# A Conformer convolution taken in two halves of 256 tokens, with the first half's layer norm and projection placed inside the second half's blocks

## The reference, cut to what matters

```python
hn = rms_norm(h, norm1_g[1])
u = hn @ w_pw1 + b_pw1                              # 1024 -> 2048
u = u[..., :1024] * jax.nn.sigmoid(u[..., 1024:])   # the gate
u = depthwise_conv(u, w_dw, width 31, causal) + b_dw
m, var = mean and variance of u over the 1024 channels of a token
u = (u - m) * lax.rsqrt(var + 1e-5) * ln_g + ln_b   # layer norm
u = silu(u)
h = h + u @ w_pw2 + b_pw2                           # the projection
```

## Time and profile before

| | |
|---|---|
| median of 3 runs | 1392.17 us |
| the profiled execution's own time | 1388.63 us |
| its span in the trace | 1386.9 us |
| granted TensorE clock, mean over the span | 0.931 of full |
| TensorE matmuls busy | 1145.5 us, 83% of the span |
| VectorE busy | 538.4 us, 39% |
| ScalarE busy | 382.7 us, 28% |
| GpSimd busy | 248.7 us, 18% |
| bytes moved by DMA | 271.85 MB |

### The profile page before, as it was taken

How to read it: one execution, slowest core, us unless ns; L and a number is a source line. 1 busy time by engine, 2 the same in 40 slices (tenths; PEclk the granted TensorE clock), 3 DMA queues, 4 the chain that set the end, 5 groups by cost and what they waited for, 6 DMA issues and landing times.

```text
span 1386.9 us, 27835 instructions
## 1 busy us (share of the span) xinstructions
PE 1145.5 (83%) x11810; PEld 624.7 (45%) x11810; DVE 538.4 (39%) x951; ACT 382.7 (28%) x727; POOL 248.7 (18%) x250
## 2 busy tenths in 40 slices
PE   5978889999999889869987882999449869988781
PEld 2345556555555464535544441444114535544440
DVE  6833545544545432331111114489971231111114
ACT  3223243334333312211111112355551211111112
POOL 2000000000000000412221110388820412221210
PEclk9999999999999999969999996999769979999996
DMA  6042110110101333489999996326200489999985
GB/s 157 3 49 4 52 51 7 47 29 26 51 6 48 148 131 111 168 331 421 420 421 422 422 385 251 109 61 218 101 0 20 153 345 421 421 421 422 422 358 206
DMA packets 149115, 271.85 MB, mean 196 GB/s; under 512 B 62178, under 2 KB 106210, under 8 KB 131584
## 3 DMA queue, kind: packets, MB, share of 16 engines
q1 hardware_dynamic: 136960, 240.68, 46.1%
q0 software_dynamic: 10880, 21.00, 4.0%
q10 hardware_dynamic: 1152, 8.39, 1.5%
HBM read 263.73 MB, written 23.07 MB: 207 GB/s over the span
## 4 chain that ended last, share of the span: by engine, by line
PE 61%; DMA 15%; DVE 9%; POOL 4%; issue 4%; SPq 4%; ACT 2%; POOLq 0%; DVEq 0%; ACTq 0%
PE psum L1212 13%; DMA big<-in_moe_w_up_dram 11%; PE psum L807 11%; PE psum L1685 8%; PE psum L1398 5%; POOL big L1888 4%; PE psum L820 4%; PE psum L1388 2%; DVE psum L1990 2%; SPq L352 2%; PE psum L1908 2%; DMA conv_w<-in_moe_w_up_dram 2%; PE psum L1367 2%; DVE h L911 1%; PE psum L786 1%
## 5 line engine op out<-in xcount | busy, mean ns | idle before, releaser
L807 PE MATMUL psum<-big 128*64 128x256 f32 x1728 | 220.3, 400 | 46.0 <-DMA big<-in_moe_w_up_dram 32.9
L1212 PE MATMUL psum<-big 128*128 128x512 f32 x384 | 198.3, 635 | 2.8 <-ACT big L1248 2.8
L807 PEld LDWEIGHTS psum<-big 128*64 128x64 f32 x1728 | 121.9, 142 | 130.6 <-DMA big<-in_moe_w_up_dram 44.6
L882 DVE TENSOR_TENSOR big<-big,psum 128x128 f32<-128x128 f32 x64 | 18.4, 288 | 332.9 <-ACT big L848 332.9
L721 POOL TENSOR_SCALAR big<-big 128x1024 f32<-128x1024 f32 x8 | 22.8, 2848 | 633.6 <-PE psum L460 633.5
L749 POOL DMA_INDIRECT chosen<-big x64 | 63.7, 995 | 353.0 <-ACT big L858 139.9
L820 PE MATMUL psum<-big 128*64 128x512 f32 x512 | 120.8, 592 | 1.2 <-ACT big L853 1.2
L1685 PE MATMUL psum<-big 128*128 128x512 f32 x256 | 116.7, 609 | 5.6 <-ACT big L1960 5.6
L1888 POOL TENSOR_TENSOR big<-big 128x512 f32<-128x512 f32 x88 | 111.8, 1271 | 43.7 <-ACT big L1947 32.2
L1908 PE MATMUL psum<-big,conv_w 128*128 128x512 f32 x256 | 110.4, 593 | 2.1 <-ACT big L418 1.2
L1541 ACT COPY big<-psum 128x512 f32<-128x512 f32 x96 | 57.2, 622 | 156.7 <-PE psum L1398 81.5
(11 more groups left out here) (248 smaller groups left out, 1339.6 us busy)
## 6 DMA issues: line engine op xcount, KB each, us to landing
big<-in_moe_w_down_dram SPq DMA_DIRECT2D x64, 1024.0 KB, 23.7
big<-in_moe_w_gate_dram SPq DMA_DIRECT2D x54, 1024.0 KB, 19.7
big<-in_moe_w_up_dram SPq DMA_DIRECT2D x54, 1024.0 KB, 23.7
big<-in_rwkv_w_rkv_dram SPq DMA_DIRECT2D x24, 512.0 KB, 5.0
conv_w<-in_moe_w_gate_dram SPq DMA_DIRECT2D x10, 1024.0 KB, 21.4
conv_w<-in_moe_w_up_dram SPq DMA_DIRECT2D x10, 1024.0 KB, 22.4
conv_w<-in_conv_w_pw_dram SPq DMA_DIRECT2D x16, 512.0 KB, 5.1
big<-chosen ACTq DMA_DIRECT2D x8, 1024.0 KB, 8.0
```

What stands on the lines that cost most here:

```text
L807: last = nc.tensor.matmul(o[half * SLOTS:(half + 1) * SLOTS, 0:F_EXP].rearrange("p (u f) -> p u f", u=2), m.xT[e // 2 % 2][:, c, (e % 2) * ...
L1212: last = nc.tensor.matmul(bank[b], m.w[:, n, c, :], x[:, c, :], start=(c == 0), stop=(c == C - 1))
```

## The change

The stage runs over 16 units instead of 8 blocks: unit `i` is channel block `i % 8` of the tokens of half `i // 8`, and every operation on a row covers 256 tokens. The gated rows `u` of all eight blocks are kept (30 pad columns and 512 tokens each), since a block's second half needs the last tokens of its first. `w1` is loaded twice, once for each half. The value and the gate of a unit share one PSUM bank.

VectorE runs the first half's centring after unit 8, adds the epsilon after unit 9 and scales after unit 10. ScalarE squares after unit 9's products, takes the root after unit 10's and SiLU after unit 11's. TensorE puts the first half's sums and its projection (token tiles 0 and 1) between the matmuls of the later units. The second half has its norm after unit 15, and its sums stand on TensorE ahead of channel blocks 5 and 6 of the projection of tiles 0 and 1.

Further: three matmuls on a token tile of `h` (into a bank that is overwritten) stand ahead of the stage on TensorE; the first unit's matmuls stand ahead of the fourth tile's transposes; the bias is added to `h` by GpSimd after unit 15, no longer by VectorE; the loads of the router's parameters and of experts 0 and 1 are issued within the second half's units.

```diff
-        def pe_mix_out(m, pe, src, wts, src_ready, after, begun=0):
+        def pe_mix_out(m, pe, src, wts, src_ready, after, begun=0, at_chunk=None, second=0):
...
             for c in range(C):
+                if at_chunk:
+                    at_chunk(c)
                 pe.wait_ge(src_ready, c + 1)
...
             for t in range(2, TT):
                 pe.wait_ge(m.mixed, t - 1)
+                if t == 2 and second:
+                    pe.wait_ge(src_ready, second)
...
-            for q in range(2, C):
-                sp.wait_ge(m.up_ps, q - 1)
-                sp_conv_w1(m, sp, q, q % 2)
...
+            for i in range(2, CONV_UNITS):
+                sp.wait_ge(m.up_ps, i - 1)
+                sp_conv_w1(m, sp, i % C, i % 2)
+                if i == C:
...
+                    sp_moe_params(moe[1], sp)
+                if i in (C + 1, C + 3):
+                    sp_load_both(moe[1], sp, (i - C) // 2)
...
+            pool.wait_ge(m.bias_in, 16)
+            for t in range(TT):
+                nc.gpsimd.tensor_tensor(h[:, t, :], h[:, t, :], m.g_row, ALU.add).then_inc(m.biased, 1)
...
+        def up_bank(i):
+            return bank[i] if i < 2 else bank[2 + i % 2]
...
+            pe.wait_ge(moe[0].h_step, 5)
+            for _ in range(3):
+                nc.tensor.matmul(bank[0], ident[:], h[:, 0, 0:512], start=True, stop=True)
...
+            def up(i):
+                b, n = i % 2, i // C
...
+                if i >= 2:
+                    pe.wait_ge(m.gated, i - 1)
                 for u in range(2):
                     for c in range(C):
...
+                        last = nc.tensor.matmul(up_bank(i)[:, part(u)], m.w1[b][:, c, u, :], m.hnT[:, c, part(n)],
...
+            for t in range(TT - 1):
+                pe_norm_columns(m, pe, t)
+            up(0)
+            pe_norm_columns(m, pe, TT - 1)
+            for i in range(1, C + 2):
+                up(i)
             pe.wait_ge(m.mean_of_ready, 1)
...
+            mean(0)
+            up(C + 2)
+            up(C + 3)
+            variance(0)
+            up(C + 4)
+            up(C + 5)
             pe.wait_ge(m.w2_in, 16)
+
+            def at_chunk(c):
+                if c == 1:
+                    up(C + 6)
+                if c == 3:
+                    up(C + 7)
+                if c == 5:
+                    mean(1)
+                if c == 6:
+                    variance(1)
...
+                if i == C + 1:
+                    squares(0)
+                if i == C + 2:
+                    root(0)
+                if i == C + 3:
+                    silu(0)
+            squares(1)
+            root(1)
+            silu(1)
...
+            for i in range(CONV_UNITS):
+                convolve(i)
+                if i == C:
+                    dve.wait_ge(m.co_ready, C)
+                    centre(0)
+                if i == C + 1:
+                    spread(0)
+                if i == C + 2:
+                    scale(0)
+            dve.wait_ge(m.co_ready, CONV_UNITS)
+            centre(1)
+            spread(1)
+            scale(1)
```

More of the change, by code:

```diff
@@ L1916, in pe_conv, with mean @@
[L1916 to L1921, removed]
-            pe.wait_ge(m.w2_in, 16)
-            pe_mix_out(m, pe, m.co, [m.w2[:, c] for c in range(C)], m.act_ready, moe[1])
+            def mean(n):
+                pe.wait_ge(m.gated, (C + 1) * (n + 1) - 2 * n)
+                for q in range(C):
+                    pe.wait_ge(m.co_ready, C * n + q + 1)
+                    last = nc.tensor.matmul(bank[2 * n][:, 0:HALF], m.mean_of, m.co[:, q, part(n)], start=(q == 0),
+                                            stop=(q == C - 1))
+                last.then_inc(m.mean_ps, 1)
@@ new lines, in variance @@
+            def variance(n):
+                for q in range(C):
+                    pe.wait_ge(m.sq_ready, C * n + q + 1)
+                    last = nc.tensor.matmul(bank[1 + 2 * n][:, 0:HALF], m.mean_of, m.sq[q], start=(q == 0),
+                                            stop=(q == C - 1))
+                last.then_inc(m.var_ps, 1)
+            pe.wait_ge(consts_ready, 2)
+            for t in range(TT - 1):
+                pe_norm_columns(m, pe, t)
+            up(0)
+            pe_norm_columns(m, pe, TT - 1)
@@ L1925, in act_conv @@
+            pe_mix_out(m, pe, m.co, [m.w2[:, c] for c in range(C)], m.act_ready, moe[1], at_chunk=at_chunk,
+                       second=2 * C)
         def act_conv(m, act, tile_ready):
@@ new lines, in squares, with root @@
+            def squares(n):
+                for q in range(C):
+                    act.wait_ge(m.centred, C * n + q + 1)
+                    nc.scalar.activation(m.sq[q], m.co[:, q, part(n)], ACT.Square).then_inc(m.sq_ready, 1)
+            def root(n):
+                rs = m.rs[:, part(n)]
+                nc.scalar.preload_act_table_set("natural_log_exp_and_others")
+                act.wait_ge(m.rs_step, 3 * n + 1)
+                nc.scalar.activation(rs, rs, ACT.Ln).then_inc(m.rs_step, 1)
+                act.wait_ge(m.rs_step, 3 * n + 2)
+                nc.scalar.activation(rs, rs, ACT.Exp, scale=-0.5).then_inc(m.rs_step, 1)
@@ new lines, in spread, with scale @@
+            def spread(n):
+                dve.wait_ge(m.var_ps, n + 1)
+                nc.vector.tensor_scalar(m.rs[:, part(n)], bank[1 + 2 * n][:, 0:HALF], LN_EPS, None,
+                                        ALU.add).then_inc(m.rs_step, 1)
+            def scale(n):
+                dve.wait_ge(m.rs_step, 3 * n + 3)
+                for q in range(C):
+                    nc.vector.tensor_tensor(m.co[:, q, part(n)], m.co[:, q, part(n)], m.rs[:, part(n)],
+                                            ALU.mult).then_inc(m.normed_, 1)
@@ L2017, in dve_conv @@
+            gate(0)
+            for i in range(CONV_UNITS):
+                convolve(i)
[10 more added lines that the diff above has]
+            scale(1)
             dve.wait_ge(m.biased, TT)
```

159 lines of the change are left out of this document (68 added, 91 removed).

## The result

| | before | after |
|---|---|---|
| median, 20 runs each | 1390.41 us | 1396.64 us |
| ratio, 95% interval | | 1.0046 [1.0031, 1.0060] |
| span of the profiled execution | 1386.9 us | 1395.5 us |
| L911's start to first gate | 36.5 us | 31.3 us |
| L911's start to the last combine | 167.9 us | 202.9 us |

L911 is the first combination of the first expert stage's results, where the last mixer's input begins. The mark is the start of VectorE's add of tile 1's projection, 1066.25 before, 1074.94 after. The forecast was 4.5 us less; the time is 6.2 us more by the medians (0.46% by the ratio), within the range of 1378 to 1397, but on the other side of zero.

A forecast was written before the change was run, and what follows sets the result against it. Bound by a GpSimd-VectorE wait loop, 15.94 us per block, then a serial 49.8 us tail. Last mean record 28.3 us later, 32.8 gained behind it: -4.5, so 1387.7 us from 1392.17; range 1378 to 1397.

The forecast's parts named there:

- contention in the norm of the first half: Sixteen VectorE centrings and scalings beside GpSimd adds in the units: 0.19 us extra per 256 columns, 3.0 us in all.
- Rival 1: VectorE operations with two SBUF inputs stand still while GpSimd reads: 11.7 us in units, 2 in tail, +6.2 sum; chance 0.10.
- the rival's point of decision: Extra time per two-SBUF-input VectorE operation from which the full-hold case decides: 0.47 us, against 0.19 in the measured row.
- the move of the bias was worth nothing: Bias adds leaving VectorE for GpSimd after the last unit gain nothing, since they lay beside the variance.
- last combine without the nested norm: End of the sixteen half-width units with no norm inserted, 9.78 us per unit: 187.8 us from L911.
- what the nested norm adds: First half's norm inside the units: 5.8 us of longer VectorE leg plus 3.0 of contention, 8.8 us.
- last combine to mark: Tail after unit 15, with second half's norm and TensorE's channel blocks, up to tile 1's projection add: 18.0 us.
- The price of the halves: Half-width units cost more than half a block, 9.78 us against 7.97 each; 21 us by the forecast's steps.
- Rival 2: GpSimd's half-width add costs only half, 0.64 us; sum -12.4 us, 1379.8; chance with the like 0.30.
- Rival 3: TensorE idles 3 us per unit, its clock halves, and unit matmuls take 13.8 us: +5 to +15; chance 0.04.
- granted clock 1.0 up to unit 15: Sign that the forecast is right: TensorE's clock stays at its full level through all the units.
- Rival 4: Projection does not get into the units; the tail keeps up to five channel blocks, 17 us more: +12; chance 0.04.

The follow-up runs named there:

- PSUM version: Changed kernel with centring and scaling reading mean and root from PSUM, the mean's copy dropped; ratio to the kernel before 0.9940.
- bias on VectorE: Changed kernel with the four bias adds moved back from GpSimd to VectorE, behind the second half's centring; ratio to the kernel before 0.9993.
- full-width experiments: Kernel before the change with only its four bias adds moved from VectorE to GpSimd, layer norm still at 512 columns; ratio 1.0026.
- again: Changed kernel run unedited a second time as a control; ratio to the kernel before 1.0029.
- halves only: Changed kernel's half-width units and early start, but norm and projection at full width after the last unit, bias on VectorE; ratio to the kernel before 1.0136.
- PSUM version with early gate and 20/11: Mean and root read from PSUM, next unit's gate issued behind tap 11, one tap moved to VectorE; ratio to the kernel before 0.9905, repeated 0.9888.

## Why the prediction was wrong

**The term that failed is the contention in the norm of the first half.** The forecast took 3.0 us from one measured pair, 1.97 against 1.21 us, though it named the difference: GpSimd had one input in SBUF there and has two here. The sixteen operations in the units took 13.5 us against 5.5 in the PSUM version, 8.0 us of contention. Rival 1 said 11.7, one whole add each; it is nearer, and its mechanism is the true one. The operations go one per add, so that each costs the add's 0.87 us pitch and not its own 0.33 plus 0.73. That is 0.50 us extra each, and the rival's point of decision was 0.47 (0.34 with the rival's own 2 us in the tail, which that figure leaves out): the sign of the result hung on it.

The pair was also misread. The forecast took it for a slower rate, 0.74 ns more per column, and scaled it to 256 columns. The same pair occurs four times in the trace of the kernel before (timelines of VectorE and GpSimd; the third is that of the earlier trace rows):

```profile
560.03 1.97 DVE L556 TENSOR_TENSOR big<-h,big 128x1024 f32<-128x1024 f32 x1
...
575.53 1.95 DVE L556 TENSOR_TENSOR big<-h,big 128x1024 f32<-128x1024 f32 x1
...
1096.76 1.95 DVE L556 TENSOR_TENSOR big<-h,big 128x1024 f32<-128x1024 f32 x1
```

```profile
559.81 2.85 POOL L721 TENSOR_SCALAR big<-big 128x1024 f32<-128x1024 f32 x1 [549.35 <-PE psum L460]
...
575.29 2.84 POOL L721 TENSOR_SCALAR big<-big 128x1024 f32<-128x1024 f32 x1 [7.69 <-PE psum L460]
...
1096.53 2.85 POOL L721 TENSOR_SCALAR big<-big 128x1024 f32<-128x1024 f32 x1 [7.90 <-PE psum L460]
```

VectorE starts 0.22, 0.24, 0.22 and 0.23 us after GpSimd's tensor_scalar and takes 1.97, 1.95, 1.97 and 1.95 us. The later it starts, the less it loses: in all thirteen profiles of this study (47 such pairs, 0.21 to 0.24 us apart) it ends 2.18 to 2.19 us after GpSimd's start. The range of starts is narrow, but it fits a wait for a moment in GpSimd's instruction, and not a slower rate. A wait does not shrink with the columns of the one who waits.

**The second part of the same term is the tail.** Rival 1 put 2 us on the second half's centring behind the bias adds; bias on VectorE shows 1.9. The forecast said that the move of the bias was worth nothing. It looked for a reader of `h` that would wait, not for a VectorE operation that would run beside GpSimd's reads. The Trainium skill, SBUF — State Buffer, "Who interferes with whom", has the rule (two SBUF inputs against a GpSimd instruction that reads SBUF), and the PSUM, bias and full-width experiments agree with it. Its full block was set aside in the forecast on the strength of one row, in which VectorE ended first beside a tensor_scalar. Beside a tensor_tensor the block is nearly full: a held VectorE operation of 256 columns ends 0.28 us after the add, and alone it lasts 0.41.

By the forecast's own steps, in us from L911:

| step | forecast | profile (again) |
|---|---|---|
| first gate | 30.4 | 31.3 (30.5) |
| add of 256 columns | 0.73 | 0.727 |
| last combine without the nested norm | 187.8 | 188.8 (halves only) |
| what the nested norm adds | 8.8 | 14.1 (13.2) |
| last combine to mark | 18.0 | 20.2 (20.2) |
| mark | 214.6 | 223.1 (222.2) |

The first three were right to 1 us. The fourth is 8.0 of contention instead of 3.0. The fifth is the held centring, 1.9 us: with the bias on VectorE the step is 18.3. The clock phase of channel block 5 lies in it too; that block took 6.2, 5.4, 5.9 and 4.5 us in the change, its repetition, bias on VectorE and operands in PSUM. **The price of the halves was right (21 us by the forecast's steps, 20.6 measured), and so was the mechanism of the gain**, but the two nearly cancel, and 7 us in one mis-sized term turned the sign.

Rival 1's sum, +6.2 us, is also the difference of the medians, but that is luck: its two terms are 11.7 and 2 us where 8.0 and 1.9 were measured, and the mark moved by 3.9 (3.0 in the repetition). It had a chance of 0.10 on record.

The other rivals. Rival 2 (cheap adds) is out by the 727 ns. Rival 3 has a grain in it. Between units the granted clock did fall (932, 952, 987 and 1014 us), and units' matmuls took 8.6 to 10.1 us instead of 7.1, as in TensorE's timeline:

```profile
923.02 7.14 PE L1930 MATMUL psum<-big,conv_w 128*128 128x256 f32 x32 [2.89 <-DVE big L2040]
932.69 8.58 PE L1930 MATMUL psum<-big,conv_w 128*128 128x256 f32 x32 [2.52 <-DVE big L2040]
...
1014.92 10.12 PE L1930 MATMUL psum<-big,conv_w 128*128 128x256 f32 x32 [2.91 <-DVE big L2040]
```

So the forecast's sign "granted clock 1.0 up to unit 15" did not come true, but the cover held: the sigmoids idled 0.3 us in all for TensorE after the first. Rival 4 did not happen. Between the 3.9 and 3.0 us of the two profiles and the 6.2 and 3.0 us between the timed medians there is a rest of up to 2.3 us that no stretch of the traces shows; executions of one kernel differ by more.

## What to carry to other kernels

Before work is laid beside another engine's, look at what both read and not only at whether the engine is free: beside GpSimd adds, a VectorE operation on two SBUF rows cost a whole add each, while the same operation with one row left in PSUM cost nothing extra (for the mean, the copy out of PSUM was the very thing that made it slow). When a forecast is a small difference of two large terms, take the one unmeasured term at its upper bound once for the sign, and count a term as unmeasured when its only row is of another kind of instruction. Before a row is scaled, see by its other occurrences whether it shows a slower rate or a wait. When a unit is halved, reckon the pace by its closed loop and not by the busy time: 9.78 us against 7.97 came out right (9.82 measured), and so did the way to shorten it.

## What was not expected of the hardware

- How much the hold depends on GpSimd's instruction: beside a tensor_scalar of 1024 columns (one SBUF input, 2.85 us) a two-input VectorE operation of 1024 columns took 1.95 to 1.98 us instead of 1.21 and ended before it; beside a tensor_tensor (two inputs) one of 256 columns ended once per add, and one of 512 columns took up to 2.83 instead of 0.68. Whether it is the number of inputs that makes this difference, or something else in the two instructions, no run here separates.
- It has two sides: the one that starts second waits. In the profile after the change VectorE's L556 started 0.06 us ahead of the same tensor_scalar (L721), not 0.22 behind it. VectorE then took its 1.23 us, and GpSimd 3.88 instead of 2.85 (timelines of VectorE and GpSimd; to be laid beside the earlier trace rows):

```profile
1090.17 1.23 DVE L556 TENSOR_TENSOR big<-h,big 128x1024 f32<-128x1024 f32 x1
```

```profile
1090.22 3.88 POOL L721 TENSOR_SCALAR big<-big 128x1024 f32<-128x1024 f32 x1 [25.83 <-PE psum L460]
```

Five of the thirteen profiles have this order at that place, all five with 3.88 or 3.89 us. It lies behind the mark, where the two executions take the same 320.6 us with this order and with the other. The wait is thus no property of VectorE. The adds beside the centrings lost nothing (eleven took 9.43 us with the centring beside them and 9.44 without, unit 13); there VectorE's operation had only 0.14 us left when the next add started. Where it had more left, GpSimd lost by it: with 0.32 us left a bias add took 2.52 us instead of 2.34, with 0.59 left (beside the full-width centring) 2.79, and with 1.17 left the tensor_scalar lost 1.04. So the four bias adds took 9.63 us beside the centring, 10.15 beside the full-width one, and 9.28 in the PSUM version with early gate and 20/11.
- The granted clock fell to 0.5 within 2.5 us without matmuls (ahead of the unit at 932.69, which took 8.58 us) and stayed at 1.0 over 2.9 us (ahead of the one at 923.02, 7.14 us). So the idle time alone does not tell what a unit will cost.
